# Attention output of a hybrid RG-LRU, attention and FFN layer: channels on the partitions instead of tokens

## The chip, the cores and the metric

One core of one Trainium2 chip runs the whole layer in one launch. The metric is the device time of an execution in microseconds (us). The engines are TensorE (PE, its weight loads PEld), VectorE (DVE), ScalarE (ACT), GpSimd (POOL) and SyncE (SP, which only issues DMAs here).

## What is computed

All is float32, for 256 tokens and a model width of 1024.

```python
h = rms_norm(x, mix_norm_g)
xr, yg, q, k, v = split(h @ w_in)                  # 512 columns each
y_lru = rg_lru(causal_conv(xr)) * gelu(yg)
q, k = rms_norm per head (8 heads of 64)
p = softmax(q k^T / 8 - slope[h] * distance, causal) # 256 keys: one block, its own
y_attn = p @ v
mixed = [rms_norm(y_lru, lru_out_g), rms_norm(y_attn, attn_out_g)]
x = x + mixed @ w_out
up = causal_conv(rms_norm(x) @ w_up)
x = x + (gelu(gate) * val) @ w_down                # inner width 2816
```

## The kernel before

Every engine has its own program, written out by hand; semaphores tie them together. The weights come as a stream of "units" of 128x1024 through six double buffers (`raw`). Each unit is split into two fp32r parts, and a product takes three matmuls (hi by hi, hi by lo, lo by hi; helper `three`, L957, L958, L961). The high part `w_hi` is made by ACT (`hi`, L336), or for units 17 to 22 by DVE (L625); DVE makes the low part `w_lo` for all (`lo`, L629). PE waits for a unit's low part by `split(u)`. The numbers: `U_V` = 16 to 19 are v's weights, `U_O` = 20 to 27 those of w_out (20 to 23 multiply the LRU's channels, 24 to 27 the attention's), 28 and up the FFN's.

Attention, in the order that matters here. Scores have queries on the partitions: per head one product of 128 queries by 128 keys and one of 128 by 256 (`KEYS`, tile half `m`). DVE adds the distance term (`shift(h)`, L724), ACT takes the exponential and sums each row (`exps(h)`, L411, `row_sum`), PE transposes the three 128x128 pieces of a head (`transpose_p(h)`, L1046) and ACT copies them out (`p_out(h)`, L417). The programs interleave these steps, by hand, with the units of w_in: PE issues `y_unit(3)`, `transpose_p(4)`, `transpose_p(5)`, v's first unit, `transpose_p(6)`, `transpose_p(7)`, v's other units. `probs` has five slots, so `shift(h)` of heads 5 to 7 waits for `transpose_p(h - 5)`.

Then the part that the diff touches. The output product has p transposed as the stationary and v as the moving operand (64 columns per head): 8 matmuls for queries 0 to 127 (L1145), 16 for queries 128 to 255 (L1151, L1152), into one bank each, tokens on the partitions. Among them stand `y_sums` (L1109: the squares of the LRU's output, summed over the channels by a column of ones) and `y_broadcast` (L1116: 1/rms put on a diagonal by DVE, L637 and L638, and spread over the partitions by ones). DVE then scales the attention output by the rows' reciprocal sums (L810), ACT squares it (L498) and takes the root (L500), DVE scales again (L819), PE transposes it into channels (`transpose_a`, L1134, before unit 23), ACT and DVE make `mix_hi` and `mix_lo` (L505, L825). The LRU's own four chunks come from `lru_norm(c)` (L797, L799, L800).

The w_out products (`out_piece`) wait for chunk kc of `mix_ready`: units 20 to 23 run one after the other over five output pieces, then units 24 to 27 for pieces 0 and 1, and for pieces 2, 3 and 4. DVE adds pieces to x (`f_add`, L837) after the low parts of units 26 to 29; the FFN norm, `transpose_f` (L1171) and the FFN (L1203, L1207, L957 to L961) follow.

## Time and profile before

| what | value |
|---|---|
| median of 3 runs | 302.09 us (301.57 to 302.38) |
| profiled execution, its own time | 302.12 us |
| its span | 300.4 us |
| granted TensorE clock, mean | 0.999 |
| PE busy (share of the span) | 293.8 us (98%) |
| DVE busy | 241.6 us (80%) |
| ACT busy | 201.4 us (67%) |
| POOL busy | 3.9 us (1%) |
| chain that ended last, PE's share | 91% |

The span is the time from the first to the last instruction in the trace; the execution's own time has 1.7 us more around it. Matmul records are pipelined: one record lasts longer than the distance to the next start, so rates are read from the starts. A plain float32 matmul appears as two records, a transpose as one.

### The profile page before, as it was taken

Reading aid. Unit: us, or ns where it says so; the run is one execution under the profiler, and the core shown is the slowest. Engines: PE = TensorE matmul, PEld = TensorE weight load, DVE = VectorE, ACT = ScalarE, POOL = GpSimd, SP = SyncE. Lnnn points to the kernel's source line nnn. Section 1 sums busy time; section 2 is a strip of 40 time slices with the busy share of each in tenths; the row PEclk is TensorE's granted clock in tenths of the full one; section 3 lists DMA queues with packets and bytes.
Section 4 is the critical chain, followed back from the end, with each engine's and each line's share of the span. In section 5 each row is a group of like instructions: output and inputs, shape, how many; then the busy total and the mean of one; then the engine's idle time right before and its main releaser. Section 6 shows DMA issues by size and latency. Waiting matters only on the chain.

```text
span 300.4 us, 4975 instructions
## 1 busy us (share of the span) xinstructions
PE 293.8 (98%) x1656; PEld 255.4 (85%) x1656; DVE 241.6 (80%) x432; ACT 201.4 (67%) x371; POOL 3.9 (1%) x21
## 2 busy tenths in 40 slices
PE   8899999999999999999999999999999999999995
PEld 8688999898998888888888888888888888888884
DVE  2898497798989766999878888888888888888864
ACT  6875498998665377877666677666666666766540
POOL 4000000000000000000000000000000000000000
PEclk9999999999999999999999999999999999999999
DMA  7999942033305810466554546383654544300003
GB/s 245 429 422 422 380 151 103 39 140 140 142 0 187 309 68 2 153 242 259 226 205 146 190 149 254 140 279 140 245 173 166 194 163 180 135 0 0 0 0 140
DMA packets 7983, 52.22 MB, mean 174 GB/s; under 512 B 896, under 2 KB 896, under 8 KB 2080
## 3 DMA queue, kind: packets, MB, share of 16 engines
q1 hardware_dynamic: 7776, 51.38, 45.4%
q0 software_dynamic: 192, 0.64, 0.5%
q8 instruction: 9, 0.15, 0.2%
q14 instruction: 6, 0.05, 0.0%
HBM read 50.98 MB, written 1.05 MB: 173 GB/s over the span
## 4 chain that ended last, share of the span: by engine, by line
PE 91%; DVE 3%; DMA 2%; ACT 2%; issue 0%; SPq 0%; ACTq 0%
PE bank L1203 27%; PE bank L957 15%; PE bank L958 14%; PE bank L961 14%; PE bank L1207 14%; DMA raw<-in_stream_dram 2%; PE bank L1033 1%; DVE x_tok L949 1%; ACT p_T L513 1%; PE bank L1046 1%; DVE h_both L862 1%; PE bank L1152 1%; PE bank L1151 1%; PE bank L1022 1%; PE bank L1145 1%; PE bank L1053 1%
## 5 line engine op out<-in xcount | busy, mean ns | idle before, releaser
L629 DVE TENSOR_TENSOR w_lo<-raw,w_hi 128x1024 fp32r<-128x1024 f32 x93 | 110.9, 1220 | 8.1 <-ACT w_hi L336 7.4
L336 ACT ACTIVATE w_hi<-raw 128x1024 fp32r<-128x1024 f32 x87 | 89.0, 1053 | 5.8 <-PE bank L961 4.2
L1203 PE MATMUL bank<-h_both,w_hi 128*128 128x512 f32 x352 | 87.8, 391 | 0.3 <-DVE h_both L862 0.3
L1203 PEld LDWEIGHTS bank<-h_both,w_hi 128*128 128x128 f32 x352 | 64.6, 188 | 13.0 <-issue 0.5
L1207 PEld LDWEIGHTS bank<-h_both,w_lo 128*128 128x128 f32 x352 | 48.0, 190 | 3.4
L1207 PE MATMUL bank<-h_both,w_lo 128*128 128x256 f32 x352 | 49.1, 282 | 0.0
L554 ACT ACTIVATE tanh_a<-bank 128x256 f32<-128x256 f32 x44 | 16.8, 383 | 42.6 <-PE bank L1207 42.4
L957 PE MATMUL bank<-w_hi,act_hi 128*128 128x512 f32 x88 | 34.5, 392 | 0.0
L958 PE MATMUL bank<-w_lo,act_hi 128*128 128x512 f32 x88 | 34.5, 392 | 0.0
L961 PE MATMUL bank<-w_hi,act_lo 128*128 128x512 f32 x88 | 34.2, 389 | 0.0
L887 DVE TENSOR_TENSOR ygate<-bank,tanh_a 128x256 f32<-128x256 f32 x44 | 18.5, 420 | 12.6 <-ACT tanh_a L554 12.5
L562 ACT ACTIVATE xc<-ygate,par 128x256 f32<-128x256 f32 x44 | 26.2, 596 | 2.3 <-DVE ygate L887 2.1
L898 DVE SCALAR_TENSOR_TENSOR xc<-ygate,par,xc 128x254 f32<-128x254 f32 x44 | 21.3, 483 | 5.1 <-DVE xc L894 0.2
L894 DVE SCALAR_TENSOR_TENSOR xc<-ygate,par,xc 128x255 f32<-128x255 f32 x44 | 21.1, 480 | 3.4 <-ACT xc L562 3.2
L957 PE MATMUL bank<-w_hi,h_both 128*128 128x512 f32 x48 | 19.0, 395 | 1.4 <-DVE h_both L661 1.4
L961 PEld LDWEIGHTS bank<-w_hi,act_lo 128*128 128x128 f32 x88 | 16.5, 188 | 3.6
L957 PEld LDWEIGHTS bank<-w_hi,act_hi 128*128 128x128 f32 x88 | 16.6, 189 | 3.0
L958 PEld LDWEIGHTS bank<-w_lo,act_hi 128*128 128x128 f32 x88 | 16.6, 189 | 2.6
L961 PE MATMUL bank<-w_hi,h_both 128*128 128x512 f32 x48 | 18.7, 390 | 0.0
L957 PE MATMUL bank<-h_both,w_hi 128*128 128x256 f32 x64 | 18.7, 292 | 0.0
L958 PE MATMUL bank<-w_lo,h_both 128*128 128x512 f32 x48 | 18.7, 389 | 0.0
L961 PE MATMUL bank<-h_both,w_lo 128*128 128x256 f32 x64 | 18.1, 283 | 0.0
(163 smaller groups left out, 387.7 us busy)
## 6 DMA issues: line engine op xcount, KB each, us to landing
raw<-in_stream_dram SPq DMA_DIRECT2D x46, 1024.0 KB, 4.8
x_tok<-in_x_dram SPq DMA_DIRECT2D x2, 512.0 KB, 3.7
raw<-in_stream_dram SPq DMA_DIRECT2D x2, 512.0 KB, 7.5
out_dram<-x_tok SPq DMA_DIRECT2D x4, 256.0 KB, 2.1
p_T<-in_gates_dram POOLq DMA_DIRECT2D x1, 512.0 KB, 9.6
par<-in_params_dram POOLq DMA_DIRECT2D x1, 117.0 KB, 4.7
```

What stands on the lines that cost most here:

```text
L336: act.activation(w_hi[u % RING][:, :], raw_unit(u), ACT.Copy).then_inc(hi_done, 1)
L554: act.activation(cross[which][s % 2], up_bank(s, which)[:, SEQ:2 * SEQ], ACT.Copy).then_inc(cross_out, 1)
L562: act.activation((conv_g, conv_v)[which][s % 2], joined[which][s % 2], ACT.Identity, bias=par[:, bass.ds(col + FFN_B, 1)], scale=par[:, ba ...
L629: dve.tensor_tensor(w_lo[u % RING][:, :], raw_unit(u), w_hi[u % RING][:, :].bitcast(F32), ALU.subtract).then_inc(lo_done, 1)
L887: dve.tensor_tensor(joined[which][s % 2], up_bank(s, which)[:, 0:SEQ], cross[which][s % 2], ALU.add).then_inc((joined_g, joined_v)[which], 1)
L894: dve.scalar_tensor_tensor(acc[:, 1:SEQ], joined[which][s % 2][:, 0:SEQ - 1], par[:, bass.ds(col + (FFN_W + 2 * STEPS), 1)], acc[:, 1:SEQ] ...
L898: dve.scalar_tensor_tensor(acc[:, 2:SEQ], joined[which][s % 2][:, 0:SEQ - 2], par[:, bass.ds(col + FFN_W, 1)], acc[:, 2:SEQ], ALU.mult, AL ...
L957: pe.matmul(acc, lhs_hi, rhs_hi, start=first, stop=False)
L958: pe.matmul(acc, lhs_hi, rhs_lo, start=False, stop=False)
L961: return pe.matmul(acc, lhs_lo, rhs_hi, start=False, stop=last)
L1203: pe.matmul(acc[:, :], whi[:, kc, :], h_both[:, kc, :, :].rearrange("p b t -> p (b t)"), start=kc == 0, stop=False)
L1207: ins = pe.matmul(acc[:, 0:SEQ], wlo[:, kc, :], h_hi[:, kc, :], start=False, stop=kc == KC - 1)
```

## The change

The output product is turned round. v is now the stationary operand (64 columns of a head), p transposed the moving one, with 256 queries for keys 0 to 127 and 128 queries for keys 128 to 255. An even head writes partitions 0 to 63 of its bank, an odd head partitions 64 to 127. So the attention output has its channels on the partitions from the start, and `transpose_a` goes. A row of probabilities is now along the output's free axis, so the rows' sums can't be divided out afterwards: GpSimd scales the probabilities before they are transposed, by reciprocals that DVE takes for two heads at a time (`row_reciprocals`), and `transpose_p` waits for `probs_scaled`. Both norms over channels change form: DVE sums the squares of four chunks, one matmul with a 128x128 block of ones sums over the partitions and spreads the sum to all of them, ACT takes the root and DVE the reciprocal on 128x256 (before: on 128x1). `a_sums` stands ahead of unit 22. DVE scales the attention's four chunks into `tanh_a`, ACT copies them to `mix_hi`, DVE subtracts for `mix_lo`. ACT's unit 27 moves behind those copies.

```diff
-y_sq_sum = gate_r[:, 0, :]
+y_sq_sum, y_rms, y_rows = (gate_r[:, c, :] for c in range(3))
+a_sq_sum, a_rms, a_rows = (gate_i[:, c, :] for c in range(3))
...
-Y_NORM, O_BANK, A_T = bank[5], (bank[4], bank[2]), bank[4:6]
+Y_SUM, A_SUM, A_ACC = bank[5][:, 0:SEQ], bank[5][:, SEQ:2 * SEQ], (bank[4], bank[2])
...
+def a_at(c):
+    return A_ACC[c // 2][:, SEQ * (c % 2):SEQ * (c % 2 + 1)]
...
+    pool.wait_ge(dist_done, TT + HEADS)
+    for h in range(HEADS):
+        pool.wait_ge(row_rec_done, h // 2 + 1)
+        for m in range(TT):
+            part = probs[h % P_SLOTS][:, KEY_AT[m]:KEY_AT[m] + KEYS[m]]
+            pool.tensor_scalar(part, part, row_rec[:, h, m:m + 1], None, ALU.mult).then_inc(probs_scaled, 1)
...
     act.wait_ge(y_sum, 1)
-    act.activation(y_rms, Y_NORM[:, 0:TT], ACT.Sqrt, bias=eps, scale=1.0 / LRU_WIDTH).then_inc(y_rms_done, 1)
-    his(23, 24, 25)
-    for m in range(TT):
-        act.wait_ge(attn_out, m + 1)
-        act.activation(sq_tok, y_attn[m], ACT.Square, accum_out=a_ss[:, m:m + 1]).then_inc(a_sq, 1)
-        act.wait_ge(a_sq, m + 1)
-        act.activation(a_rms[:, m:m + 1], a_ss[:, m:m + 1], ACT.Sqrt, bias=eps,
-                       scale=1.0 / ATTN_WIDTH).then_inc(a_rms_done, 1)
-    his(26, 27)
+    act.activation(y_rms, Y_SUM, ACT.Sqrt, bias=eps, scale=1.0 / LRU_WIDTH).then_inc(y_rms_done, 1)
+    his(23)
+    for j in range(2):
+        act.wait_ge(o_done, j + 1)
+        act.activation(flat(q_T)[:, 512 * j:512 * (j + 1)], A_ACC[j][:, :], ACT.Square).then_inc(a_sq, 1)
+    his(24, 25)
+    act.wait_ge(a_sum, 1)
+    act.activation(a_rms, A_SUM, ACT.Sqrt, bias=eps, scale=1.0 / ATTN_WIDTH).then_inc(a_rms_done, 1)
+    his(26)
     for c in range(LC):
-        act.wait_ge(aT, c // 2 + 1)
-        act.activation(mix_hi[:, LC + c, :], A_T[c // 2][:, SEQ * (c % 2):SEQ * (c % 2 + 1)], ACT.Copy,
-                       scale=par[:, ATTN_G + c:ATTN_G + c + 1]).then_inc(aT_hi, 1)
+        act.wait_ge(a_scaled, c + 1)
+        act.activation(mix_hi[:, LC + c, :], tanh_a[:, c, :], ACT.Copy).then_inc(a_hi, 1)
+    his(27)
...
+    def row_reciprocals(h):
+        dve.wait_ge(probs_done, TT * (h + 2))
+        dve.reciprocal(row_rec[:, h:h + 2, :], row_sum[:, h:h + 2, :]).then_inc(row_rec_done, 1)
...
     conv_rest(3)
+    row_reciprocals(0)
     los(16)
+    row_reciprocals(2)
...
     shift(7)
-    los(19, 20)
+    row_reciprocals(4)
+    los(19)
+    row_reciprocals(6)
+    los(20)
...
-    dve.wait_ge(consts, 2)
     dve.wait_ge(y_rms_done, 1)
-    for m in range(TT):
-        make_diag(y_rms, y_rstd, m, y_diag)
-    dve.wait_ge(y_bc, 1)
+    link(dve.reciprocal(y_rows, y_rms))
     def lru_norm(c):
         link(dve.scalar_tensor_tensor(decay[:, c, :], ygate[:, c, :], par[:, LRU_G + c:LRU_G + c + 1],
-                                      Y_NORM[:, SEQ:2 * SEQ], ALU.mult, ALU.mult))
+                                      y_rows, ALU.mult, ALU.mult))
         link(dve.tensor_copy(mix_hi[:, c, :], decay[:, c, :]))
         dve.tensor_tensor(mix_lo[:, c, :], decay[:, c, :], mix_hi[:, c, :].bitcast(F32),
                           ALU.subtract).then_inc(mix_ready, 1)
     lru_norm(0)
     lru_norm(1)
-    dve.wait_ge(probs_done, HEADS * TT)
-    link(dve.reciprocal(row_rec, row_sum))
-    dve.wait_ge(o_done, 1)
-    for m in range(TT):
-        dve.tensor_tensor(y_attn[m].rearrange("p (h d) -> p h d", h=HEADS),
-                          O_BANK[m][:, :].rearrange("p (h d) -> p h d", h=HEADS),
-                          row_rec[:, :, m:m + 1].to_broadcast([P, HEADS, HEAD_DIM]),
-                          ALU.mult).then_inc(attn_out, 1)
+    dve.wait_ge(a_sq, 2)
+    dve.tensor_reduce(a_sq_sum, q_T[:, :, :].rearrange("p c t -> p t c"), AX_X, ALU.add).then_inc(a_chunks, 1)
     lru_norm(2)
     los(23)
-    for m in range(TT):
-        dve.wait_ge(a_rms_done, m + 1)
-        link(dve.reciprocal(a_rstd[:, m:m + 1], a_rms[:, m:m + 1]))
-        dve.tensor_scalar(y_attn[m], y_attn[m], a_rstd[:, m:m + 1], None, ALU.mult).then_inc(a_normed, 1)
     lru_norm(3)
+    dve.wait_ge(a_rms_done, 1)
+    link(dve.reciprocal(a_rows, a_rms))
+    for c in range(LC):
+        dve.scalar_tensor_tensor(tanh_a[:, c, :], a_at(c), par[:, ATTN_G + c:ATTN_G + c + 1], a_rows,
+                                 ALU.mult, ALU.mult).then_inc(a_scaled, 1)
     los(24, 25)
-    for j in range(2):
-        dve.wait_ge(aT_hi, 2 * j + 2)
-        for c in (2 * j, 2 * j + 1):
-            dve.scalar_tensor_tensor(mix_lo[:, LC + c, :], A_T[j][:, SEQ * (c % 2):SEQ * (c % 2 + 1)],
-                                     par[:, ATTN_G + c:ATTN_G + c + 1],
-                                     mix_hi[:, LC + c, :].bitcast(F32),
-                                     ALU.mult, ALU.subtract).then_inc(mix_ready, 1)
+    for c in range(LC):
+        dve.wait_ge(a_hi, c + 1)
+        dve.tensor_tensor(mix_lo[:, LC + c, :], tanh_a[:, c, :], mix_hi[:, LC + c, :].bitcast(F32),
+                          ALU.subtract).then_inc(mix_ready, 1)
     los(26, 27)
...
     def transpose_p(h):
-        pe.wait_ge(probs_done, TT * (h + 1))
+        pe.wait_ge(probs_scaled, TT * (h + 1))
...
     def y_sums():
         pe.wait_ge(y_chunks, 1)
-        for m in range(TT):
-            ins = pe.matmul(Y_NORM[:, m:m + 1], y_sq_sum[:, P * m:P * (m + 1)], ones[:, 0:1],
-                            start=True, stop=True)
-        ins.then_inc(y_sum, 1)
-    def y_broadcast():
-        pe.wait_ge(y_diag, TT)
-        for m in range(TT):
-            ins = pe.matmul(Y_NORM[:, SEQ + P * m:SEQ + P * (m + 1)], ones[:, :], diag[:, m, :],
-                            start=True, stop=True)
-        ins.then_inc(y_bc, 1)
+        pe.matmul(Y_SUM, ones[:, :], y_sq_sum, start=True, stop=True).then_inc(y_sum, 1)
+    def a_sums():
+        pe.wait_ge(a_chunks, 1)
+        pe.matmul(A_SUM, ones[:, :], a_sq_sum, start=True, stop=True).then_inc(a_sum, 1)
...
-    def transpose_a():
-        pe.wait_ge(a_normed, TT)
-        pe.wait_ge(mix_ready, LC)
-        for c in range(LC):
-            for m in range(TT):
-                at = SEQ * (c % 2) + P * m
-                ins = pe.transpose(A_T[c // 2][:, at:at + P], y_attn[m][:, P * c:P * (c + 1)], ident[:, :])
-            if c % 2 == 1:
-                ins.then_inc(aT, 1)
-    def head(h):
-        return slice(HEAD_DIM * h, HEAD_DIM * (h + 1))
+    def attend(h, m):
+        half, v_head = slice(HEAD_DIM * (h % 2), HEAD_DIM * (h % 2 + 1)), slice(HEAD_DIM * h, HEAD_DIM * (h + 1))
+        queries, at = slice(P * m, SEQ), KEY_AT[m] if m == 0 else 2 * P
+        return pe.matmul(a_at(h // 2)[half, queries], v_tok[:, m, v_head], p_T[:, h, at:at + SEQ - P * m],
+                         start=m == 0 and h // 2 % 2 == 0, stop=m == TT - 1, skip_group_check=True)
     pe.wait_ge(pT_read, HEADS)
     pe.wait_ge(v_ready, 1)
     for h in range(HEADS):
-        pe.matmul(O_BANK[0][:, head(h)], p_T[:, h, 0:P], v_tok[:, 0, head(h)], start=True, stop=True)
+        attend(h, 0)
     pe.wait_ge(v_ready, TT)
     y_sums()
     for h in range(HEADS):
-        if h == HEADS // 2:
-            y_broadcast()
-        pe.matmul(O_BANK[1][:, head(h)], p_T[:, h, P:2 * P], v_tok[:, 0, head(h)], start=True, stop=False)
-        ins = pe.matmul(O_BANK[1][:, head(h)], p_T[:, h, 2 * P:3 * P], v_tok[:, 1, head(h)],
-                        start=False, stop=True)
-    ins.then_inc(o_done, 1)
+        ins = attend(h, 1)
+        if h % 4 == 3:
+            ins.then_inc(o_done, 1)
     pe.wait_ge(shifted, HEADS)
     for j in range(LC):
-        if j == LC - 1:
-            transpose_a()
+        if j == LC - 2:
+            a_sums()
         u = U_O + j
         split(u)
```

The order of PE's instructions from the end of v's last unit to the start of unit 20, before:

```order
L961 MATMUL bank<-w_hi,h_both 128x512
L1145 MATMUL bank<-v_tok,p_T 128x64 x8
L1109 MATMUL bank<-ones,gate_r 128x1 x2
L1151 MATMUL bank<-v_tok,p_T 128x64
L1152 MATMUL bank<-v_tok,p_T 128x64
...
L1116 MATMUL bank<-diag,ones 128x128 x2
...
L957 MATMUL bank<-w_hi,mix_hi 128x512
```

and with the change:

```order
L959 MATMUL bank<-w_hi,h_both 128x512
L1124 MATMUL bank<-p_T,v_tok 64x256 x8
L1106 MATMUL bank<-gate_r,ones 128x256
L1124 MATMUL bank<-p_T,v_tok 64x128 x8
L955 MATMUL bank<-w_hi,mix_hi 128x512
```

Twenty-four matmuls of 64 columns have become eight of 256 and eight of 128; the sum of the LRU's squares stands behind the first eight in both, and the broadcast is gone.

The order on DVE from the last `shift` to the first product of the LRU's root, with the change (before, the two rows of L732 are not there):

```order
L725 ISA qk_tok,small<-bank,neg_dist 128x256
L725 ISA small 128x1
L732 RECIPROCAL small<-small 128x4
L631 CAST w_hi<-raw 128x1024
L635 TENSOR_TENSOR w_lo<-raw,w_hi 128x1024
L732 RECIPROCAL small<-small 128x4
L631 CAST w_hi<-raw 128x1024
L635 TENSOR_TENSOR w_lo<-raw,w_hi 128x1024
L788 TENSOR_TENSOR gate_r<-tanh_a,gate_i 128x1024
```

The reciprocals for heads 4 and 5 stand ahead of unit 19's split, those for heads 6 and 7 ahead of unit 20's. GpSimd's instructions for these heads (two per head, of 128x128 and 128x256) become free to run there.

DVE from the fourth chunk of the LRU to the FFN's first addition, before:

```order
L800 TENSOR_TENSOR mix_lo<-decay,mix_hi 128x256
L629 TENSOR_TENSOR w_lo<-raw,w_hi 128x1024 x2
L825 SCALAR_TENSOR_TENSOR mix_lo<-bank,par,mix_hi 128x256 x4
L629 TENSOR_TENSOR w_lo<-raw,w_hi 128x1024 x4
L837 TENSOR_TENSOR x_tok<-x_tok,bank 128x512 x2
```

and with the change:

```order
L807 TENSOR_TENSOR mix_lo<-decay,mix_hi 128x256
L818 RECIPROCAL gate_i<-gate_i 128x256
L820 SCALAR_TENSOR_TENSOR tanh_a<-bank,par,gate_i 128x256 x4
L635 TENSOR_TENSOR w_lo<-raw,w_hi 128x1024 x2
L825 TENSOR_TENSOR mix_lo<-tanh_a,mix_hi 128x256 x4
L635 TENSOR_TENSOR w_lo<-raw,w_hi 128x1024 x4
L835 TENSOR_TENSOR x_tok<-x_tok,bank 128x512 x2
```

A reciprocal and four scalings are new ahead of the splits of units 24 and 25; behind them the order is the same.

## Rows read from the trace of the kernel before

**Rows 1.** Stretch, its length; busy PE, PEld, DVE, ACT, POOL; clock; DMA.

```profile
0.00:5.00 5.00, 3.92 (x18) 3.92 (x19) 0.00 (x0) 2.32 (x3) 3.25 (x19) 1.00 0.61 229
57.90:94.90 37.00, 37.00 (x245) 32.87 (x244) 32.51 (x59) 26.80 (x57) 0.00 (x0) 1.00 0.31 114
114.10:300.40 186.30, 183.12 (x968) 157.57 (x968) 153.00 (x251) 120.50 (x203) 0.00 (x0) 1.00 0.42 152
```

**Rows 2.** Timeline of ACT: the end of head 5's exponentials; v's first copy.

```profile
64.79 0.19 ACT L411 ACTIVATION_READ_ACCUMULATOR qk_tok<-qk_tok,small 128x1 f32 x1
...
78.50 0.58 ACT L491 ACTIVATE v_tok<-bank 128x512 f32<-128x512 f32 x1
```

**Rows 3.** Timeline of DVE behind the last shift.

```profile
66.38 0.69 DVE L625 CAST w_hi<-raw 128x1024 fp32r<-128x1024 f32 x1
67.10 1.23 DVE L629 TENSOR_TENSOR w_lo<-raw,w_hi 128x1024 fp32r<-128x1024 f32 x1
...
70.96 1.22 DVE L778 TENSOR_TENSOR gate_r<-tanh_a,gate_i 128x1024 f32<-128x1024 f32 x1 [0.77 <-ACT tanh_a L475]
```

**Rows 4.** Groups of DVE by form: count | busy us, mean ns | idle.

```profile
L797 DVE SCALAR_TENSOR_TENSOR decay<-ygate,par,bank 128x256 f32<-128x256 f32 x4 | 1.9, 476 | 1.1 <-PE bank L1116 1.1
L800 DVE TENSOR_TENSOR mix_lo<-decay,mix_hi 128x256 fp32r<-128x256 f32 x4 | 1.7, 426 | 0.1
L799 DVE CAST mix_hi<-decay 128x256 fp32r<-128x256 f32 x4 | 1.2, 294 | 0.1
L697 DVE RECIPROCAL small<-small 128x16 f32<-128x16 f32 x2 | 0.5, 253 | 0.8 <-ACT small L396 0.8
L752 DVE RECIPROCAL small<-small 128x4 f32<-128x4 f32 x1 | 0.2, 178 | 0.0
```

**Rows 5.** Timeline of POOL, which computes nothing after 5.2 us.

```profile
2.82 0.29 POOL L316 TENSOR_SCALAR_AFFINE_SELECT neg_dist<-neg_dist 128x128 f32<-128x128 f32 x1
...
3.56 0.40 POOL L316 TENSOR_SCALAR_AFFINE_SELECT neg_dist<-neg_dist 128x256 f32<-128x256 f32 x1
```

**Rows 6.** Timeline of PE: start, us, line, names, form, idle before.

```profile
42.86 0.93 PE L1033 MATMUL bank<-k_T,q_T 64*128 64x128 f32 x8
...
54.17 0.92 PE L1033 MATMUL bank<-k_T,q_T 64*128 64x128 f32 x4
...
67.15 0.81 PE L1046 MATMUL bank<-ident,qk_tok 128*128 128x128 f32 x6
67.72 0.47 PE L957 MATMUL bank<-w_hi,h_both 128*128 128x512 f32 x1
...
79.41 1.89 PE L1145 MATMUL bank<-v_tok,p_T 128*128 128x64 f32 x16
81.14 0.56 PE L1109 MATMUL bank<-ones,gate_r 128*128 128x1 f32 x4
...
85.58 0.48 PE L957 MATMUL bank<-w_hi,mix_hi 128*128 128x512 f32 x1
...
94.01 1.04 PE L1134 MATMUL bank<-ident,q_T 128*128 128x128 f32 x8
94.80 0.47 PE L957 MATMUL bank<-w_hi,mix_hi 128*128 128x512 f32 x1
...
97.66 0.40 PE L957 MATMUL bank<-w_hi,mix_hi 128*128 128x512 f32 x1
```

**Rows 7.** The chain that ended last: one float32 matmul, 256 columns (two records).

```profile
50.79 0.43 PE bank L1053 x2
```

**Rows 8.** Groups of ACT by form: 256 columns from PSUM.

```profile
L434 ACT ACTIVATE k_T<-bank,par 128x256 f32<-128x256 f32 x4 | 2.0, 494 | 0.0
```

**Rows 9.** Timeline of DVE from the attention's low parts to the first addition.

```profile
95.52 1.66 DVE L825 SCALAR_TENSOR_TENSOR mix_lo<-bank,par,mix_hi 128x256 fp32r<-128x256 f32 x4 [0.56 <-ACT mix_hi L505]
97.10 4.62 DVE L629 TENSOR_TENSOR w_lo<-raw,w_hi 128x1024 fp32r<-128x1024 f32 x4
102.65 1.37 DVE L837 TENSOR_TENSOR x_tok<-x_tok,bank 128x512 f32<-128x512 f32 x2 [0.94 <-PE bank L961]
```

More of the change, by code:

```diff
@@ L164, in build_layer @@
         q_scale = small[:, 76:80]
-        y_rms, y_rstd = small[:, 80:82], small[:, 82:84]
-        a_ss, a_rms, a_rstd = small[:, 84:86], small[:, 86:88], small[:, 88:90]
         f_ss, f_sum, f_rms, f_rstd = small[:, 200:205], small[:, 94:96], small[:, 96:98], small[:, 98:100]
@@ L195, in build_layer @@
         ygate_done, y_done, y_sq, y_chunks = sem("ygate_done"), sem("y_done"), sem("y_sq"), sem("y_chunks")
-        y_sum, y_rms_done, y_diag, y_bc = sem("y_sum"), sem("y_rms_done"), sem("y_diag"), sem("y_bc")
+        y_sum, y_rms_done = sem("y_sum"), sem("y_rms_done")
         mix_ready = sem("mix_ready")
@@ L634, in los @@
                     lo(u)
-            def make_diag(rms, rstd, m, done):
-                link(dve.reciprocal(rstd[:, m:m + 1], rms[:, m:m + 1]))
-                dve.tensor_scalar(diag[:, m, :], ident[:, :], rstd[:, m:m + 1], None, ALU.mult).then_inc(done, 1)
             def x_reciprocal(m):
```

9 lines of the change are left out of this document (3 added, 6 removed).

## The prediction

> **What bounds the kernel now.** I read the page's shares first: PE has 91% of the chain that ended last. The table by stretch then shows where PE has slack. From 57.90 to 94.90 us it is busy for all 37.00 us, and in the FFN for 183.12 of 186.30 us; the granted clock is 1.00, that is 2.4 GHz, everywhere [rows 1]. So PE sets the pace, but only just: the timelines of DVE and ACT over the same stretch show work that arrives a few tenths of a microsecond ahead of PE. In such a place fewer PE instructions gain nothing unless what PE waits for comes earlier too. I therefore walk along the change and ask at each PE step: when does PE get there, and when is its input ready? The FFN behind 114 us is left as it is; whatever shift its first matmul has, the end has.
>
> **Scaling on GpSimd.** New work sits between exponentials and transposes. For heads 0 to 3 it has time: DVE's program has their reciprocals around unit 16's split, ahead of a chain of a dozen small instructions and of `shift(4)`, and PE transposes them after that. Heads 4 and 5 are tight. Head 5's exponentials end at 64.98 [rows 2], but the reciprocal stands in DVE's program behind the last shift, so it starts at 66.38 [rows 3] and takes 0.18 us, the length for 4 columns [rows 4]: 66.56. GpSimd then has four instructions. Their price isn't in the trace; the nearest rows are another one-input GpSimd instruction, 0.29 us for 128 columns and 0.40 for 256 [rows 5], 1.38 us for the two heads. PE wants head 4 at 67.15 and head 5 half of 0.57 us later, at 67.44 [rows 6].
>
> GpSimd's timeline has no compute beside DVE's: in the first 5 us DVE is busy for 0.00 us [rows 1], and later GpSimd computes nothing. So whether the two disturb each other isn't shown. Low end: not at all; head 5 is ready at 66.60 + 1.38 = 67.98, and PE is 0.58 us late. High end: every one of the four waits behind one of DVE's (CAST 0.69, low part 1.23 [rows 3]). I take a value between: GpSimd waits once, for the CAST that starts with it, and DVE's next large instruction waits for the four. It is the first end plus the nearest row's length, the CAST of 0.69 us [rows 3] that starts in the moment in which GpSimd becomes free to; the four stand in one program with no wait between heads' halves, so once begun they can run on. Then head 5 is ready at 66.56 + 0.69 + 0.04 + 1.38 = 68.67, PE 1.27 us late. DVE loses 1.38 us here, as much again for heads 6 and 7 behind the next CAST, and 0.36 for two reciprocals: 3.12 us, of which 0.77 us of waiting before L778 [rows 3] absorb a part. L778 and all behind it move by 2.35 us, through the scan, the squares and ScalarE's table load, to v's first copy: 78.50 + 2.35 + 0.58 = 81.43 [rows 2]. PE wants that at 79.41 [rows 6] and starts at 81.47: **+2.06 us**. The first lateness is contained in this one.
>
> The rule that speaks against this change is in the Trainium skill, SBUF — State Buffer, "Who interferes with whom": VectorE's second pair of SBUF ports is GpSimd's only one, and an instruction that has it keeps it to its end while the other waits. It names casts and instructions with two SBUF inputs. No row here shows it; by it any of the eight instructions from head 4 on may be held up, which is the rival "turn by turn" below.
>
> **Output product and the LRU's sum.** A float32 product of 256 columns takes 0.43 us [rows 7]. The score products show that two heads on different halves of the array run at once: eight records last 0.93 us where four last 0.92 [rows 6]. Those are row halves, here it is column halves; I take them as equal. The first eight products cost 4 x 0.43 and some 0.06 for the first load, 1.78 us, as much as the 1.73 they replace (79.41 to 81.14), since each has twice the queries. So the LRU's sum starts at 83.25. Then a chain follows that PE can't shorten: sum over 256 columns 0.43 and, since a record ends 0.16 after the next may start, 83.84; ACT's root 0.49 [rows 8] + 0.04, 84.37; the reciprocal; three instructions of `lru_norm(0)`, 0.48 + 0.29 + 0.43 [rows 4] and 0.04 each between: 1.32.
>
> The reciprocal of 128x256 is the second price that isn't in the trace. From 4 to 16 columns it rises from 178 to 253 ns [rows 4], 6.25 ns a column; 240 more give 1.75 us. Low end: that of a CAST of the same size, 0.29 us. I take 1.75, the same instruction's own slope. It ends at 86.16, the first chunk at 87.48, unit 20 starts at 87.52 instead of 85.58: **+1.94**. PE's other eight products (128 columns, 4 x 0.22) end near 84.7, so about 2.8 us of PE stand idle here. What the product saves (24 matmuls of 64 columns at 0.22 us are 5.2 us, now 1.78 + 0.88), and the broadcast's two matmuls, lie in that gap and gain nothing.
>
> By the Trainium skill, VectorE: DVE Perf Modes, "First, the fixed hardware budget", the divider repeats eight times, and at 0.96 GHz a column would cost 8.3 ns, an estimate of 2.3 us; the sum would be 1.1 us higher, since two such reciprocals are on the path. The rows here say 6.25 ns.
>
> **Units 20 to 23.** They take 97.66 - 85.58 = 12.08 us before [rows 6]. `transpose_a` goes (94.80 - 94.01 = 0.79), `a_sums` comes (0.43): 11.72, end at 99.24, **+1.58**. For `a_sums` nothing is late: the reduction ends near 91, PE is there at 87.52 + 2 x 2.82 = 93.17 (two of four units at 11.29 / 4).
>
> **From the attention's sum to its chunks.** Before, mix_lo of the first chunk was ready at 95.9 for a start at 97.66. Now: sum 93.17 + 0.59 = 93.76, root 94.29, reciprocal 1.79, 96.08, four scalings at 0.40 (L825's pitch [rows 9]) 97.72, two low parts 2.35, 100.07, then the first mix_lo, 0.43. ACT's copies are done by then. Unit 24 starts at 100.54 instead of 97.66: **+2.88**, a new wait of 1.3 us.
>
> **The first addition to x.** Behind its four mix_lo (1.38) DVE has four low parts, 4.62 us [rows 9]: 100.07 + 1.38 + 4.62 = 106.07. PE delivers the piece at 100.54 + (102.65 - 97.66) = 105.53, so DVE is late and its 0.94 us of waiting [rows 9] are gone. L837 starts at 106.07 instead of 102.65: **+3.42**. From there to the FFN one chain of DVE and ACT steps runs, which is not touched.
>
> The profiled execution took 302.12 us, 0.03 over the median of the runs. 302.12 + 3.4 = 305.5 us, 1.1% slower. What a measurement can tell from no change is about 0.3%, 0.9 us.
>
> **The rivals.**
> - *Side by side.* GpSimd and DVE don't disturb each other. Lateness is 0.58 us at the transposes and stays so at v's copy; all later figures are 1.48 us lower, and the addition is at +1.94: 304.1 us. For it: no row shows a conflict. Against: both work on SBUF at that moment without a pause.
> - *Turn by turn.* Each GpSimd instruction lets one of DVE's pass. After the CAST: 0.29, low part 1.23, 0.40, CAST 0.69, 0.29, low part 1.23, 0.40: head 5 is ready at 67.29 + 4.53 = 71.8, PE 4.4 us late, and the rest as above (-0.12, -0.36, +1.30, +0.54): +5.8, 307.9 us. Mixed orders lie between, 306.7 in the middle. For it: these DVE instructions are already in line when GpSimd's next one comes.
> - *Column halves one after the other.* The change doesn't do what it says: the first eight products take 3.5 us instead of 1.8. Only these count, as the sum stands behind them: +1.7 on either case, 305.8 to 307.2 us. Against: the score products' rows.
> - *Cheap reciprocals, faster.* The slope of small reciprocals doesn't hold for wide ones. With 0.29 us instead of 1.75 two steps on the path lose 2 x 1.46 us; with GpSimd side by side, 1.94 - 2.92 = -1.0: 301.1 us. It decides from a reciprocal below 0.8 us on; with the one turn of my forecast it only reaches +0.5, no change. The place to see it is the start of unit 20, at 84.6. Against: the same instruction's rows at 4 and 16 columns.
> - *The clock falls.* PE waits for nothing from 57.90 to 94.90 us now [rows 1]; the new 2.8 us of idle before unit 20 could lower its clock. At 1.2 GHz unit 20's 2.87 us would double: +2.9 more, 308.4 us. No row here has the lower level.
>
> **How the numbers follow.** Forecast 0.38, side by side 0.25, turn by turn or mixed 0.17, column halves 0.07, the clock 0.03: all slower, 0.90. Cheap reciprocals 0.10, of which half with a turn (no change) and half without (faster). I round to slower 0.88, within 0.3% 0.06, faster 0.06. The range reaches from somewhat below side by side, 303.5, to the end of turn by turn, 307.9; cheap reciprocals and the clock are left out. If the forecast holds, 304.9 to 306.1.
>
> **What would show it.** The new reciprocals of 128x256 at 1.75 us; PE's first record of head 5's transposes near 68.7, and w_lo of unit 19 starting only when GpSimd's four are done; v's first copy near 80.9; the first eight products done in 1.8 us; PE idle of about 2.8 us before unit 20 and 1.3 us before unit 24, with DVE as releaser; L837's successor at 106.1 without a wait. Wrong would be: no idle on PE before unit 20, reciprocals below 0.8 us, or an FFN of another length than 186.3 us.

## The result: 311.1 us, 3.0% slower, and the profile after

| | before | changed |
|---|---|---|
| median of 4 runs each | 302.24 us (301.57 to 302.82) | 311.10 us (310.63 to 311.49) |
| ratio, with its 95% interval | | 1.030 (1.027 to 1.033) |
| span of the profiled execution | 300.4 us | 309.0 us |
| granted clock, mean | 0.999 | 0.989 |

The forecast was 305.5 us with a range to 307.9. The sign was right, the size less than half of what came: 3.4 us instead of 8.9, or of 8.6 between the two spans (in its profiled execution the changed kernel's first unit started 0.23 us earlier, at 10.29 instead of 10.52 us). In some executions of a kernel PE is at 1.2 GHz in one or two stretches more than in others, which is worth some 1.5 us each, and the mean clock given beside a time tells it. First the stretches of the changed kernel, with the columns of [rows 1]:

```profile
57.90:66.93 9.03, 9.03 (x73) 7.98 (x71) 7.99 (x20) 8.78 (x27) 1.99 (x2) 1.00 0.32 116
66.93:71.77 4.84, 0.70 (x5) 0.31 (x3) 3.38 (x4) 1.13 (x5) 4.84 (x5) 0.94 0.46 156
71.77:74.62 2.85, 2.85 (x9) 2.37 (x10) 0.00 (x0) 1.88 (x3) 2.85 (x4) 0.50 0.25 104
74.62:85.20 10.58, 10.58 (x50) 8.51 (x49) 9.39 (x11) 7.23 (x10) 0.06 (x1) 1.00 0.12 35
85.20:91.52 6.32, 3.60 (x35) 2.24 (x35) 4.17 (x6) 4.30 (x7) 0.00 (x0) 1.00 0.26 110
91.69:95.10 3.41, 3.41 (x9) 2.67 (x9) 3.31 (x6) 0.41 (x1) 0.00 (x0) 0.50 0.00 0
95.10:106.06 10.96, 9.78 (x55) 8.38 (x54) 8.88 (x15) 5.31 (x9) 0.00 (x0) 1.00 0.25 96
122.67:309.00 186.33, 183.17 (x968) 157.70 (x968) 152.94 (x251) 120.25 (x203) 0.00 (x0) 1.00 0.43 152
```

Three things stand in it. From 66.93 to 71.77 PE works 0.70 us of 4.84 while GpSimd (POOL, the fifth pair) works throughout. Twice the clock is 0.50, that is 1.2 GHz, and each time PE has waited just before (the first time it falls some 0.6 us before the wait ends, which is why the row above has 0.94). And the FFN has its old length, 186.33 against 186.30 us [rows 1], so all of the loss is made ahead of 122.67 us. PE's timeline gives the places; the brackets are its idle time and what ended it:

```profile
69.39 0.55 PE L1044 MATMUL bank<-ident,qk_tok 128*128 128x128 f32 x3 [2.31 <-POOL qk_tok L333]
71.77 0.90 PE L1044 MATMUL bank<-ident,qk_tok 128*128 128x128 f32 x3 [1.83 <-POOL qk_tok L333]
...
85.20 1.95 PE L1124 MATMUL bank<-p_T,v_tok 128*64 128x256 f32 x16
87.08 0.70 PE L1106 MATMUL bank<-gate_r,ones 128*128 128x256 f32 x2
...
91.52 0.62 PE L955 MATMUL bank<-w_hi,mix_hi 128*128 128x512 f32 x1 [2.72 <-DVE mix_lo L807]
...
98.73 0.60 PE L1110 MATMUL bank<-gate_i,ones 128*128 128x256 f32 x2
...
106.06 0.47 PE L955 MATMUL bank<-w_hi,mix_hi 128*128 128x512 f32 x1 [1.18 <-DVE mix_lo L825]
...
122.67 0.71 PE L1185 MATMUL bank<-h_both,w_hi 128*128 128x512 f32 x2 [0.28 <-DVE h_both L860]
```

And VectorE's, at the shifts and at the two wide reciprocals and the first addition:

```profile
66.15 0.17 DVE L732 RECIPROCAL small<-small 128x4 f32<-128x4 f32 x1
66.23 0.66 DVE L631 CAST w_hi<-raw 128x1024 fp32r<-128x1024 f32 x1
66.93 1.27 DVE L635 TENSOR_TENSOR w_lo<-raw,w_hi 128x1024 fp32r<-128x1024 f32 x1
68.13 0.16 DVE L732 RECIPROCAL small<-small 128x4 f32<-128x4 f32 x1
68.22 0.87 DVE L631 CAST w_hi<-raw 128x1024 fp32r<-128x1024 f32 x1
69.12 1.23 DVE L635 TENSOR_TENSOR w_lo<-raw,w_hi 128x1024 fp32r<-128x1024 f32 x1
75.60 1.23 DVE L788 TENSOR_TENSOR gate_r<-tanh_a,gate_i 128x1024 f32<-128x1024 f32 x1 [5.25 <-ACT tanh_a L482]
...
88.32 1.75 DVE L801 RECIPROCAL gate_r<-gate_r 128x256 f32<-128x256 f32 x1 [2.04 <-ACT gate_r L500]
...
99.87 1.75 DVE L818 RECIPROCAL gate_i<-gate_i 128x256 f32<-128x256 f32 x1 [1.95 <-ACT gate_i L507]
...
111.38 1.28 DVE L835 TENSOR_TENSOR x_tok<-x_tok,bank 128x512 f32<-128x512 f32 x2
```

And ScalarE's copy of v's first half, for which the forecast let the output product wait. It ends at 84.55 us; PE is busy throughout from 71.77 to 85.20 us and doesn't wait for it:

```profile
83.95 0.60 ACT L498 ACTIVATE v_tok<-bank 128x512 f32<-128x512 f32 x1 [0.71 <-PE bank L959]
```

Set side by side at PE's and VectorE's marks, the 8.6 us are made like this ([rows 6, 9] for before; 67.44 is head 5's transposes as in the prediction):

| from, to | before | changed | difference | forecast |
|---|---|---|---|---|
| start to head 5's transposes | 67.44 | 71.77 | +4.33 | +1.27 |
| to the output product | 11.97 | 13.43 | +1.46 | +0.79 |
| to unit 20 | 6.17 | 6.32 | +0.15 | -0.12 |
| to unit 24 | 12.08 | 14.54 | +2.46 | +0.94 |
| to the first addition | 4.99 | 5.32 | +0.33 | +0.54 |
| to the FFN | 11.40 | 11.29 | -0.11 | 0 |
| sum | | | +8.62 | +3.42 |

Two rows hold what the forecast lacks, beside 0.67 us in the second: 3.06 us at the transposes and 1.52 in units 20 to 23.

### The profile page after: what moved, and what is told of

It reads as the page before. It is cut to its first block, busy times and chain, and to the rows that moved or that the text cites. A ratio compares the mean times of both kernels' runs of the same rounds, so it can differ in the third digit from the quotient of the medians.

```text
span 309.0 us, 4930 instructions
## 1 busy us (share of the span) xinstructions
PE 294.4 (95%) x1628; PEld 253.2 (82%) x1628; DVE 245.4 (79%) x432; ACT 200.9 (65%) x368; POOL 20.0 (6%) x37
## 4 chain that ended last, share of the span: by engine, by line
PE 77%; DVE 9%; ACT 8%; DMA 2%; POOL 1%; issue 1%; POOLq 0%; SPq 0%; DVEq 0%; ACTq 0%
PE bank L1185 26%; PE bank L1189 14%; PE bank L955 12%; PE bank L956 12%; PE bank L959 12%; DVE w_lo L635 3%; DMA raw<-in_stream_dram 2%; ACT qk_tok L418 1%; POOL qk_tok L333 1%; DVE x_tok L947 1%; ACT p_T L519 1%; DVE h_both L860 1%; ACT w_hi L343 1%; PE bank L1124 1%; DVE gate_r L801 1%
## 5 line engine op out<-in xcount | busy, mean ns | idle before, releaser
L1189 PE MATMUL bank<-h_both,w_lo 128*128 128x256 f32 x352 | 49.1, 283 | 0.0
L955 PE MATMUL bank<-w_hi,h_both 128*128 128x512 f32 x48 | 19.5, 407 | 1.1 <-DVE h_both L662 1.1
L959 PE MATMUL bank<-w_hi,h_both 128*128 128x512 f32 x48 | 19.0, 396 | 0.0
L955 PE MATMUL bank<-w_hi,mix_hi 128*128 128x512 f32 (+1 forms) x40 | 15.0, 374 | 3.9 <-DVE mix_lo L807 2.7
```

What stands on the lines that cost most here:

```text
L955: pe.matmul(acc, lhs_hi, rhs_hi, start=first, stop=False)
L959: return pe.matmul(acc, lhs_lo, rhs_hi, start=False, stop=last)
L1189: ins = pe.matmul(acc[:, 0:SEQ], wlo[:, kc, :], h_hi[:, kc, :], start=False, stop=kc == KC - 1)
```

## The experiments

All ratios are to the kernel before, run on the same chip beside each. The expectation that stands ahead of each result was on record before the run.

| kernel | median, us | ratio (95% interval) |
|---|---|---|
| changed | 311.10 | 1.030 (1.027 to 1.033) |
| no scaling | 304.61 | 1.009 (1.006 to 1.011) |
| VectorE scales heads 4 to 7 | 306.26 | 1.012 (1.008 to 1.016) |
| PE's gaps filled | 308.20 | 1.023 (1.020 to 1.027) |
| reciprocals of 128x256 as copies | 307.36 | 1.021 (1.016 to 1.026) |
| VectorE quiet beside GpSimd | 310.37 | 1.026 (1.019 to 1.032) |
| LRU's sum first | 308.66 | 1.022 (1.015 to 1.028) |
| head 4's reciprocal early | 309.28 | 1.025 (1.018 to 1.031) |
| before, GpSimd beside it | 303.57 | 1.004 (1.001 to 1.007) |
| before, PE waits for GpSimd | 305.40 | 1.010 (1.007 to 1.012) |
| rebuilt | 303.87 | 1.006 (1.004 to 1.007) |
| rebuilt, gap filled | 303.70 | 1.005 (1.003 to 1.006) |
| rebuilt, ScalarE shares | 301.83 | 0.999 (0.997 to 1.001) |

**No scaling**, from the changed kernel.

```diff
-            for h in range(HEADS):
-                pool.wait_ge(row_rec_done, h // 2 + 1)
...
+            pass
...
-                pe.wait_ge(probs_scaled, TT * (h + 1))
+                pe.wait_ge(probs_done, TT * (h + 1))
```

> GpSimd's sixteen multiplications are left out, the transposes wait for the exponentials alone (so the probabilities stay unscaled; the reciprocals are still taken). Theory 'GpSimd late': its instructions hold PE up by 4.05 us at head 5's transposes and by the 1.2 GHz that follows, 1.7 us more. Both go: head 5's transposes at 67.7 to 67.9 us, clock 1.00 until unit 20, about 305.5 us in all. Rival 'the chains behind it decide': DVE's chain to unit 20 and to unit 24 would have made PE wait anyway, and the time stays above 309.

304.61 us, 0.9 less than expected: of the 8.9 us, 6.5 hang on GpSimd's multiplications, and the chains behind don't cover them. Everything else of the change is still in this kernel, and so are its two later waits:

```profile
85.99 0.77 PE L951 MATMUL bank<-w_hi,mix_hi 128*128 128x512 f32 x1 [2.73 <-DVE mix_lo L803]
...
100.32 0.47 PE L951 MATMUL bank<-w_hi,mix_hi 128*128 128x512 f32 x1 [1.19 <-DVE mix_lo L821]
```

**VectorE scales heads 4 to 7.**

```diff
-            for h in range(HEADS):
+            for h in range(4):
                 pool.wait_ge(row_rec_done, h // 2 + 1)
...
+                if h >= 4:
+                    dve.wait_ge(row_rec_done, h // 2 + 1)
+                    dve.wait_ge(probs_scaled, 8)
+                    for k in (h, h + 1):
+                        for m in range(TT):
+                            part = probs[k % P_SLOTS][:, KEY_AT[m]:KEY_AT[m] + KEYS[m]]
+                            dve.tensor_scalar(part, part, row_rec[:, k, m:m + 1], None,
+                                              ALU.mult).then_inc(probs_scaled, 1)
```

> Heads 4 to 7 are scaled by VectorE right behind their reciprocals, heads 0 to 3 by GpSimd as before. Theory 'GpSimd late': eight VectorE instructions of some 0.2 to 0.3 us, about 1 us of lateness for heads 4 and 5 and no fall of the clock there; 306.0 to 306.8 us. Rival 'any engine is too late here': head 5's transposes come behind 69 us, the clock falls all the same, above 308.

306.26 us, as expected. Its timeline of VectorE has the four instructions of two heads in 0.92 us from start to next start (GpSimd needed 5.3):

```profile
68.66 1.01 DVE L739 TENSOR_SCALAR qk_tok<-qk_tok,small 128x128 f32<-128x128 f32 x4
69.58 0.69 DVE L631 CAST w_hi<-raw 128x1024 fp32r<-128x1024 f32 x1
```

PE has no idle at the transposes. What the eight cost shows later, where PE waits 0.82 us for v's first copy: the wait that the forecast had for the change itself.

**VectorE quiet.** Where do GpSimd's 5.3 us for heads 4 and 5 come from?

```diff
             row_reciprocals(4)
+            row_reciprocals(6)
+            dve.wait_ge(probs_scaled, TT * HEADS)
             los(19)
-            row_reciprocals(6)
```

> VectorE waits, after the reciprocals of heads 4 to 7, until GpSimd has scaled all four, and only then splits units 19 and 20. Theory 'two causes': GpSimd's instructions take 0.60 and 0.93 us by themselves, and what stands above that in the changed kernel (2.25 us over heads 4 and 5) is waiting while VectorE's casts and subtractions run. Here all eight take 0.60 or 0.93, four of them 3.1 us in place of 5.3; head 5's transposes start near 69.5 in place of 71.77. Rival 'GpSimd is erratic by itself': durations above 1.4 us remain. The whole time says less, since VectorE's splits come later: 308.5 to 311 us.

GpSimd's groups by form from 66 to 76 us, of the changed kernel:

```profile
L333 POOL TENSOR_SCALAR qk_tok<-qk_tok,small 128x256 f32<-128x256 f32 x4 | 4.8, 1189 | 0.0
L333 POOL TENSOR_SCALAR qk_tok<-qk_tok,small 128x128 f32<-128x128 f32 x4 | 3.7, 914 | 7.0 <-DVE small L732 7.0
```

and with VectorE quiet:

```profile
L333 POOL TENSOR_SCALAR qk_tok<-qk_tok,small 128x256 f32<-128x256 f32 x4 | 3.7, 922 | 0.0
L333 POOL TENSOR_SCALAR qk_tok<-qk_tok,small 128x128 f32<-128x128 f32 x4 | 2.4, 604 | 7.0 <-DVE small L732 7.0
```

The changed kernel's instructions of this line again, with their durations in ns (least, median, most), and from its timeline the first of head 4 and the two that follow it:

```profile
L333 POOL TENSOR_SCALAR qk_tok<-qk_tok,small x16: 597/923/1992, 51.6 to 73.8; 128x128 f32<-128x128 f32 x8, 128x256 f32<-128x256 f32 x8
...
66.41 0.95 POOL L333 TENSOR_SCALAR qk_tok<-qk_tok,small 128x128 f32<-128x128 f32 x1 [7.04 <-DVE small L732]
67.35 3.47 POOL L333 TENSOR_SCALAR qk_tok<-qk_tok,small 128x256 f32<-128x256 f32 x2
```

With VectorE quiet all are at 0.60 and 0.92 us, eight in 5.94 us, so four in 2.97. In the changed kernel the second is the longest, 1.99 us, and the third has what is left, 1.50 us for 128 columns; the four take 5.30. PE's idle ahead of heads 4 and 5 falls from 2.31 + 1.83 to 0.89 + 0.93 us, by 2.32. So GpSimd's 5.30 us have two parts of like size: its own length, 2.97, and waiting beside VectorE, 5.30 - 2.97 = 2.33. Head 5's transposes start at 70.55 us; in this execution all marks ahead of them lie 1.09 us later than in the changed kernel's, which makes it 69.5, as expected. The whole gains little, 310.37, since VectorE now does its splits later: in this kernel the output product does wait for v's first copy, 1.20 us.

**Before, with GpSimd beside it**: sixteen multiplications on a tile of their own, and eight instructions of four kinds in the first microseconds.

```diff
...
+            for h in range(HEADS):
+                pool.wait_ge(probs_done, TT * (2 * (h // 2) + 2))
+                for m in range(TT):
+                    part = spare[:, KEY_AT[m]:KEY_AT[m] + KEYS[m]]
+                    if h:
+                        pool.wait_ge(spare_done, TT * (h - 1) + m + 1)
+                    pool.tensor_scalar(part, part, ones[:, 0:1], None, ALU.mult).then_inc(spare_done, 1)
```

> The kernel before, with the sixteen multiplications of GpSimd on a tile that nobody reads, each two heads' worth released by their exponentials; and eight GpSimd instructions in the first microseconds: multiplication by a column, by a constant, copy, subtraction, each on 128 and on 256 columns. Theory 'one-sided': GpSimd waits for VectorE, VectorE loses at most 0.2 us an instruction, nobody waits for the product: 302.0 to 302.6 us. Rival 'the two take turns': VectorE loses as much as GpSimd's instructions last, 1 us or more arrives at the end, above 303. In the quiet beginning 0.60 and 0.93 us for the product by a column; if a constant is much cheaper (below 0.4 for 128 columns), the column operand is the price.

GpSimd's timeline of the first part:

```profile
5.81 1.32 POOL L332 TENSOR_SCALAR spare<-spare,ones 128x128 f32<-128x128 f32 x1
7.11 1.06 POOL L333 TENSOR_SCALAR spare<-spare,ones 128x256 f32<-128x256 f32 x1
8.33 0.53 POOL L336 TENSOR_SCALAR spare<-spare 128x128 f32<-128x128 f32 x1 [0.16 <-POOL spare L333]
8.83 0.85 POOL L337 TENSOR_SCALAR spare<-spare 128x256 f32<-128x256 f32 x1
9.82 0.29 POOL L340 COPY spare<-neg_dist 128x128 f32<-128x128 f32 x1
10.06 0.59 POOL L341 COPY spare<-neg_dist 128x256 f32<-128x256 f32 x1
```

The first two ran beside VectorE and say nothing of their own length; the next two had it quiet. A constant in place of the column saves 0.07 us (0.53 and 0.85 against 0.60 and 0.92), so the column operand isn't the price: this kind of instruction is. A copy of 128 columns takes half, 0.29 us, though a CAST of VectorE's ran beside two thirds of it; that of 256 ran wholly beside VectorE.

VectorE lost more than the 0.2 us an instruction of the expectation. The low part of a half unit, beside GpSimd's two-input subtraction, took 1.06 us:

```profile
11.51 1.06 DVE L696 TENSOR_TENSOR w_lo<-raw,w_hi 128x512 fp32r<-128x512 f32 x1
```

and in the kernel before 0.68:

```profile
10.29 0.68 DVE L666 TENSOR_TENSOR w_lo<-raw,w_hi 128x512 fp32r<-128x512 f32 x1
```

The whole time missed its range too, 303.57 us. In the profiled execution the first unit started at 11.73 us instead of 10.52 (VectorE waited 1.98 us for a DMA there, before 1.03), and PE was at 1.2 GHz from 12.88 to 16.29 us. From head 4's transposes to the end it has 303.6 - 69.98 = 233.6 us against 300.4 - 67.15 = 233.25 before, so at the last four heads mere presence beside VectorE costs some 0.4 us. The ratio says 0.2 to 2.1 us for the whole kernel, the eight early instructions with it; that isn't settled closer.

**Before, with PE waiting for GpSimd**, the same sixteen, and one line more:

```diff
                 pe.wait_ge(probs_done, TT * (h + 1))
+                pe.wait_ge(spare_done, TT * (h + 1))
```

> The kernel before with GpSimd's sixteen multiplications on a tile that nobody reads, as beside it before, but now PE's transposes wait for them as they do in the change; nothing else of the change is in it. Theory 'the waits alone make most of it': GpSimd starts 1.4 us earlier than in the change, as no reciprocal stands ahead; head 5's transposes are late by some 2.3 us, head 7's by some 3.9, and the clock falls behind the wait: 306.0 to 308.0 us. Rival 'the late chains of the change are needed': PE makes the time up in the old output product, below 304.

305.40 us, 0.6 below the range. In its profile head 5's transposes waited 2.45 us, those of heads 6 and 7 didn't wait (the expectation had head 7 late by 3.9 us), and the clock fell once, for 3.4 us behind the wait. The first addition to x came at 106.36 us instead of 102.65, so the old output product made up nothing of it. Two of the four executions, at a mean clock of 1.00, took 304.51 and 304.95 us: there the wait by itself costs 2.3 to 2.8 us over the 302.16 of the kernel before on that chip. The wait for GpSimd is a loss by itself, in either kernel.

**PE's gaps filled**: unused products of 128 columns in the three gaps of PE.

```diff
             y_unit(3)
+            pe.wait_ge(shifted, HEADS)
+            warm_up(9)
             transpose_p(4)
+            warm_up(8)
             transpose_p(5)
...
             pe.wait_ge(shifted, HEADS)
+            warm_up(12)
```

> The changed kernel with unused products on PE in its three gaps: 9 and 8 of 128 columns before the transposes of heads 4 and 5, 12 before unit 20. Theory 'the clock adds to the waits': the granted clock stays 1.00 throughout, each of the two stretches of 3.4 us at 1.2 GHz gives 1.7 us back, 307.7 us. Rival 'the next wait takes it': the output product still starts earlier, but unit 24 or the first addition waits for DVE's chain so that less than 1 us arrives, above 310.

308.20 us: less than the changed kernel by 2.1 us by the ratios and by 2.8 by the spans. Its stretches, columns as above:

```profile
71.94:84.01 12.07, 12.07 (x58) 9.82 (x58) 8.42 (x9) 9.02 (x12) 2.91 (x4) 1.00 0.09 31
84.01:90.33 6.32, 6.32 (x59) 4.99 (x59) 5.12 (x8) 4.31 (x7) 0.00 (x0) 1.00 0.38 150
90.33:103.29 12.96, 11.78 (x64) 10.05 (x63) 12.40 (x20) 5.89 (x10) 0.00 (x0) 1.00 0.23 82
```

The clock is 1.00 throughout. From head 5's transposes to the product it has 12.07 us in place of 13.43, and from unit 20 to unit 24 12.96 in place of 14.54. So the clock cost 1.36 us in v's units and 1.58 us in the output's. The middle stretch is 6.32 us in both: there PE waits for VectorE, and no clock helps.

**Cheap reciprocals.**

```diff
-            link(dve.reciprocal(y_rows, y_rms))
+            link(dve.tensor_copy(y_rows, y_rms))
...
-            link(dve.reciprocal(a_rows, a_rms))
+            link(dve.tensor_copy(a_rows, a_rms))
```

> Both reciprocals of 128x256 are replaced by a copy (the sums' roots are multiplied in place of their reciprocals). Theory 'both on the path': each copy takes 0.3 us in place of 1.75, unit 20 comes 1.4 us earlier and unit 24 by 1.2 more, 308.3 us, less if the shorter gap keeps the clock at 1.00 (306.7). Rival 'the second is covered': only unit 20's 1.4 us arrive, 309.7.

307.36 us, between the two figures expected. Unit 20's wait is down from 2.72 to 1.27 us and unit 24's is gone, so both reciprocals were on the path. Behind the shorter gap unit 20 ran at 2.4 GHz (in the profiled execution; the other stretch at 1.2 GHz, at the transposes, was 6.8 us long there, twice that of the changed kernel):

```profile
90.61 0.47 PE L955 MATMUL bank<-w_hi,mix_hi 128*128 128x512 f32 x1 [1.27 <-DVE mix_lo L807]
```

**The LRU's sum first.**

```diff
-        Y_SUM, A_SUM, A_ACC = bank[5][:, 0:SEQ], bank[5][:, SEQ:2 * SEQ], (bank[4], bank[2])
+        Y_SUM, A_SUM, A_ACC = bank[7][:, SEQ:2 * SEQ], bank[5][:, SEQ:2 * SEQ], (bank[4], bank[2])
...
             pe.wait_ge(pT_read, HEADS)
+            y_sums()
             pe.wait_ge(v_ready, 1)
             for h in range(HEADS):
                 attend(h, 0)
             pe.wait_ge(v_ready, TT)
-            y_sums()
```

> The LRU's sum by ones stands ahead of the output product's first eight instead of behind them (in a free half bank). Theory 'the chain of sum, root, reciprocal and chunk ends last': it starts 1.9 us earlier less one sum of 0.43, unit 20 starts about 2 us earlier relative to the product's start, PE's idle there shrinks from 2.7 to below 1 us and the clock stays at 1.00 in units 20 to 23: 307.3 to 307.8 us. Rival 'the clock falls all the same': 309.0. Rival 'VectorE is late for the chunk anyway': above 310.

308.66 us, 0.9 above the range. The step itself did as expected: PE's wait before unit 20 is 1.06 us and the clock stays at 1.00 from there on. But in all four executions the clock came out at 0.987 or 0.988, and the profiled one shows why: around the transposes PE was at 1.2 GHz from 69.87 to 76.70 us, twice as long as in the changed kernel and as long as with the cheap reciprocals. Nothing that either edit moves stands there; why it lasted longer is open.

**Head 4's reciprocal early.**

```diff
-                pool.wait_ge(row_rec_done, h // 2 + 1)
+                pool.wait_ge(row_rec_done, (1, 1, 2, 2, 3, 4, 5, 5)[h])
...
             shift(5)
-            los(17, 18)
+            los(17)
+            row_reciprocals(4, 1)
+            los(18)
...
+            row_reciprocals(5, 1)
             shift(6)
             shift(7)
-            row_reciprocals(4)
```

> Head 4's reciprocal is taken alone right behind unit 17's split, head 5's alone ahead of the last shifts; GpSimd scales all heads as in the change. Theory 'start, not engine': GpSimd has head 4 done before head 5's exponentials end, head 5 ready by 67.3 us, PE late by 0.4 us at most, no fall of the clock there: 305.0 to 306.0 us, as without any scaling. Rival 'GpSimd itself is too slow wherever it starts': above 308.

```profile
67.68 0.55 PE L1046 MATMUL bank<-ident,qk_tok 128*128 128x128 f32 x3 [0.39 <-POOL qk_tok L333]
73.28 0.55 PE L1046 MATMUL bank<-ident,qk_tok 128*128 128x128 f32 x3 [1.66 <-POOL qk_tok L333]
88.30 0.47 PE L957 MATMUL bank<-w_hi,mix_hi 128*128 128x512 f32 x1 [2.73 <-DVE mix_lo L809]
```

309.28 us; only the profiled execution, 306.02, came near the range. Heads 4 and 5 went as expected there, 0.39 us late. What the expectation left out is heads 6 and 7: GpSimd collides with VectorE there too, and head 7's transposes wait 1.66 us, so the wait has only moved. The profiled execution had a mean clock of 1.00; the other three, at 0.987 to 0.989, took 309.18 to 310.88 us, and where their clock fell no trace shows. So both theories were half right: an earlier start helps the heads that get it, and GpSimd with some 1.5 us a head at best can't serve the last four in the time that PE gives.

**The rebuilt version.** Is there a form of this idea that is no loss?

```diff
-            for h in range(HEADS):
+            for h in range(5):
                 pool.wait_ge(row_rec_done, h // 2 + 1)
...
+            def diags(rms, rstd):
+                link(dve.reciprocal(rstd, rms))
+                for m in range(TT):
+                    dve.tensor_scalar(diag[:, m, :], ident[:, :], rstd[:, m:m + 1], None, ALU.mult).then_inc(norm_diag, 1)
...
-            link(dve.reciprocal(y_rows, y_rms))
+            diags(y_rms, y_rstd)
...
-            link(dve.reciprocal(a_rows, a_rms))
+            diags(a_rms, a_rstd)
...
+            broadcast(1, y_bc)
```

> The change with its critical places rebuilt, same result: GpSimd scales heads 0 to 4 (head 4's reciprocal early), VectorE heads 5 to 7; the row sums of squares go through one column per 128 tokens, a reciprocal of two columns, two diagonals and a broadcast product, as in the kernel before (for the attention's too), in place of the reciprocals of 128x256; v's first copy stands ahead of ScalarE's table load; unit 22's low part and unit 25's behind the chunks that PE waits for. Theory 'only the waits were wrong': transposes on time, output product at 79.4 to 79.8 us, unit 20 at 84.8 in place of 85.58, unit 24 without a wait at 96.8, clock 1.00, 301.3 us against 302.1 of before. Rival 'the saved products buy an idle PE': 1.3 us of idle before unit 20 let the clock fall there, 303 us or more.

> As the rebuilt version, with five unused products of 128 columns (1.1 us) on PE in the gap before unit 20. If the gap costs the clock there, this keeps 1.00 and gives 301.3 to 301.6 us; if not, it is equal to the rebuilt version within 0.3 us.

303.87 and 303.70 us. All scaling waits of PE are gone, and filling the gap (1.45 us of idle before unit 20, filled 0.34) changed the time by less than the intervals: that gap didn't cost the clock. But neither came to 301.3; the rival's time, 303 us or more, came without its cause. One stretch tells why, from unit 20 to the first addition, of the filled version:

```profile
85.88:105.03 19.15, 18.43 (x94) 15.29 (x95) 18.59 (x32) 6.51 (x10) 0.00 (x0) 1.00 0.34 121
```

and of the kernel before:

```profile
85.58:102.65 17.07, 17.07 (x92) 14.71 (x92) 15.27 (x27) 7.52 (x14) 0.00 (x0) 1.00 0.45 159
```

VectorE is busy for 18.59 of 19.15 us, 3.3 us more than before, and PE is no longer busy without a pause. The change takes work from PE, which had it in a place where it waits anyway, and gives some to VectorE, in the stretch in which VectorE had only 1.8 us to spare.

**ScalarE shares**, from the rebuilt version with its gap filled. The high parts of the LRU's chunks 1 to 3 and a copy go to ScalarE, which was busy for 6.51 us of the 19.15, and unit 29's low part stands behind the first additions.

```diff
+            def n_his(c):
+                act.wait_ge(n_scaled, c)
+                act.activation(mix_hi[:, c, :], decay[:, c, :], ACT.Copy).then_inc(n_hi, 1)
...
-            lru_norm(1)
+            n_scale(1)
             low(22)
+            n_low(1)
+            n_scale(2)
...
-            los(U_FFN, U_FFN + 1)
+            los(U_FFN)
             f_add(0)
             f_add(1)
             f_mean(0)
+            los(U_FFN + 1)
```

> As the rebuilt and filled version, with four unused products, and some of VectorE's work behind unit 20's start moved to ScalarE, which idles there: the high parts of the LRU's chunks 1 to 3 and the copy of the attention's broadcast row; unit 29's low part stands behind the first additions to x. Theory 'VectorE is the bound now': in the rebuilt version it has no idle from the first chunk to the first addition (105.03 us in its profile, PE delivers the piece at 102.8); 1.8 us less of it brings unit 24 without a wait, the first addition at PE's pace, and 301.2 to 301.8 us. Rival 'ScalarE answers too late': the new turns between the two engines cost what they save, 303 us or more.

```profile
86.19:103.26 17.07, 17.07 (x90) 14.71 (x91) 16.07 (x26) 8.22 (x14) 0.00 (x0) 1.00 0.38 128
```

301.83 us, ratio 0.999 (0.997 to 1.001). PE has no idle in the stretch, which is as long as before. So the idea can be had without a loss, and without a gain that can be measured. The moves to ScalarE and of unit 29's low part aren't part of the idea, and what they would do for the kernel before wasn't tried. PE's work there is the same too: two short sums and a broadcast stand where the transposes were, and the cheaper output product lies ahead of unit 20, beside the LRU's chain, which sets the pace.

## Why the prediction was right in sign and wrong in size

**The bound, right.** Fewer PE instructions gained nothing, and each loss stands at a place where PE waits for its input. The FFN kept its length.

**Scaling on GpSimd, the step that failed.** "Their price isn't in the trace; the nearest rows are another one-input GpSimd instruction", 1.38 us for two heads. They take 2.97 us when VectorE is quiet. The row was near in columns and in engine, but not in operation; by the forms above the multiplication costs about twice the select (0.60 and 0.92 against 0.29 and 0.40 us). Second, "GpSimd waits once", 0.69 us: it waited for parts of four VectorE instructions, 2.33 us. Own length and waits were off by about as much (1.59 and 1.64 us), and their sum of 3.23 us, less 0.19 by which GpSimd started earlier than forecast, is the table's 3.06 to within 0.02. The range kept a high end of 71.8 us for head 5, which is where it came (71.72), in the rival "turn by turn". That agreement is luck: the rival had the multiplications at the select's price and whole turns of VectorE's between them, and the trace has them twice as long and the waits shorter.

**VectorE's delay and the wait for v's first copy, wrong.** "DVE loses 1.38 us here": its four instructions beside GpSimd took 0.66, 1.27, 0.87 and 1.23 us against 0.69 and 1.23 [rows 3], 0.19 us in all. L788 starts 4.6 us late nevertheless, because it waits for ScalarE's root, which stands behind the copies of the late transposes. PE was just as late itself, so the wait for v's first copy, +0.79 in the forecast, didn't come. What stands in that row of the table, +1.46, is the clock: with the gaps filled it is 12.07 - 11.97 = +0.10.

**The rule on the shared ports.** The CASTs and two-input subtractions stretch GpSimd's instructions from 0.92 us to 1.99, and with VectorE quiet all return to 0.60 and 0.92. The Trainium skill, SBUF — State Buffer, "Who interferes with whom", names these two kinds among those that contend, and the trace agrees. It also has the pair kept by whoever issues first while the other is fully blocked. That is not what stands here: VectorE's second CAST started while GpSimd's instruction of 1.99 us was under way and was 0.18 us longer than the 0.69 of [rows 3], and it was GpSimd that waited for the most part.

**Output product and the LRU's sum, right.** The first eight products took 87.08 - 85.20 = 1.88 us (forecast 1.78, one after the other 3.5), so column halves do run side by side and that rival is out. The reciprocals took 1.75 us each, as forecast from the slope of the small ones; by the Trainium skill, VectorE: DVE Perf Modes, "First, the fixed hardware budget", the estimate was 2.3 us, and the measured row decides. PE's idle before unit 20 is 2.72 us (2.8). The step as a whole is +0.15 instead of -0.12.

**The clock, the second miss.** It was a rival at 0.03, for one gap, in place of a term for both. It came in both, 1.36 and 1.58 us as filling the gaps shows. The first gap was larger than forecast, because GpSimd was later; the second was forecast at its true size, and only its consequence was held for unlikely. That unit 20's 2.87 us "would double" was too much: 1.58 us arrived.

**Units 20 to 24 and the first addition, right.** A wait of 1.18 us before unit 24 (1.3) and the first addition without its old wait (bracket gone from L835). Without the clock's 1.58 us, unit 24 is at +0.88, against +0.94.

With GpSimd's true time, no wait for v's copy and the clock in both gaps the same sum is 3.42 + 3.06 - 0.79 + 1.36 + 1.58 = 8.63 us; 8.62 came. What is left in the rows, 0.1 to 0.3 us each, cancels.
